# Split memory products in the convolution stage: one product between a tile's two pointwise units, two homes for the normed memory, other turns for the loads and taps

## The reference

```python
ff = silu(h2 @ w_ffn_gate) * (h2 @ w_ffn_up)            # 1024 -> 2816
x = x + ff @ w_ffn_down

def conformer_conv(h, ...):
    u = h @ w_pw1 + b_pw1                               # 1024 -> 2048
    a, gate = split(u, 2)
    u = a * sigmoid(gate)
    u = causal depthwise convolution of u, 31 taps, + b_dw
    u = silu(layernorm(u, ln_g, ln_b))
    return u @ w_pw2 + b_pw2

def memory_cross_attention(h, mem_n, ...):              # mem_n = rmsnorm(mem, norm_memsrc_g[layer])
    k = mem_n @ w_k                                     # 256 x 1024, for each of two layers
    v = mem_n @ w_v
    ...
```

## Time and profile before

| | us |
|---|---|
| median of 3 runs (lowest, highest) | 2284.11 (2280.6, 2284.97) |
| the profiled execution, its own time | 2286.37 |
| its span, first to last instruction | 2284.6 |
| PE busy | 2227.5 (98%) |
| DVE, ACT, POOL busy | 1341.9, 975.7, 403.4 |
| mean granted clock of PE | 0.991 |

### The profile page before, as it was taken

One profiled execution on the slowest core, in us unless ns is written; L12 is line 12 of the kernel. 1 busy time (PEld: TensorE's weight loads), 2 busy tenths in 40 slices (PEclk: granted clock), 3 DMA queues, 4 the chain that ended last, 5 costly groups with the idle time before them and its releaser, 6 DMA issues.

```text
span 2284.6 us, 31292 instructions
## 1 busy us (share of the span) xinstructions
PE 2227.5 (98%) x10692; PEld 1809.7 (79%) x10692; DVE 1341.9 (59%) x1900; ACT 975.7 (43%) x1490; POOL 403.4 (18%) x336
## 2 busy tenths in 40 slices
PE   8999999999999889889999999999999999999998
PEld 6787788888888677758888888887777888888887
DVE  5567757555545867865465445485555646454455
ACT  6775644433433556653342222245444333222222
POOL 2232102110010457624040000030000404000003
PEclk9999999999999999989999999999999999999999
DMA  4222223555666665532123333332221222333332
GB/s 147 65 65 63 76 83 93 161 188 184 198 191 216 192 197 184 169 127 66 57 81 101 93 101 93 92 93 79 59 63 56 84 65 83 101 92 95 99 95 89
DMA packets 413080, 253.36 MB, mean 111 GB/s; under 512 B 14832, under 2 KB 394224, under 8 KB 412976
## 3 DMA queue, kind: packets, MB, share of 16 engines
q1 hardware_dynamic: 412080, 249.68, 36.0%
q0 software_dynamic: 896, 2.33, 0.3%
HBM read 232.56 MB, written 18.87 MB: 110 GB/s over the span
## 4 chain that ended last, share of the span: by engine, by line
PE 85%; DVE 4%; POOLq 3%; issue 2%; ACT 2%; DMA 1%; DVEq 1%; SPq 0%; ACTq 0%; POOL 0%
PE bank L1944 24%; PE bank L1946 23%; PE bank L1945 23%; POOLq L674 3%; PE bank L1924 2%; DVE m_w_lo L1253 1%; PE bank L2415 1%; PE bank L2392 1%; PE bank L2097 1%; PE bank L2521 1%; PE bank L2488 1%; DVE bank L1649 1%; PE bank L2322 1%; PE bank L2235 1%; PE bank L2237 1%
## 5 line engine op out<-in xcount | busy, mean ns | idle before, releaser
L699 ACT ACTIVATE m_w_hi<-m_raw 128x1024 fp32r<-128x1024 f32 x332 | 351.3, 1058 | 817.4 <-PE bank L1946 802.1
L1944 PE MATMUL bank<-m_h_hi,m_w_hi 128*128 128x512 f32 x1504 | 607.0, 404 | 4.4 <-DVE m_w_lo L1253 2.3
L1946 PE MATMUL bank<-m_h_hi,m_w_lo 128*128 128x512 f32 x1504 | 587.0, 390 | 0.0
L1945 PE MATMUL bank<-m_h_lo,m_w_hi 128*128 128x512 f32 x1504 | 586.3, 390 | 0.0
L1253 DVE TENSOR_TENSOR m_w_lo<-m_raw,m_w_hi 128x1024 fp32r<-128x1024 f32 x332 | 449.0, 1352 | 125.9 <-ACT m_w_hi L699 121.8
L1944 PEld LDWEIGHTS bank<-m_h_hi,m_w_hi 128*128 128x128 f32 x1504 | 282.7, 188 | 76.0 <-issue 11.3
L1946 PEld LDWEIGHTS bank<-m_h_hi,m_w_lo 128*128 128x128 f32 x1504 | 282.3, 188 | 60.1
L1945 PEld LDWEIGHTS bank<-m_h_lo,m_w_hi 128*128 128x128 f32 x1504 | 282.9, 188 | 55.5 <-issue 2.4
L1944 PE MATMUL bank<-m_f_hi,m_w_hi 128*128 128x512 f32 x688 | 269.3, 391 | 3.2 <-DVE m_w_lo L1253 3.2
L1946 PE MATMUL bank<-m_f_hi,m_w_lo 128*128 128x512 f32 x688 | 267.9, 389 | 0.0
L1945 PE MATMUL bank<-m_f_lo,m_w_hi 128*128 128x512 f32 x688 | 267.8, 389 | 0.0
(11 more groups left out here) (399 smaller groups left out, 3256.5 us busy)
## 6 DMA issues: line engine op xcount, KB each, us to landing
m_raw<-in_ff_w SPq DMA_DIRECT2D x256, 256.0 KB, 3.0
mem_low<-m_mem_raw_lo SPq DMA_DIRECT2D x32, 512.0 KB, 3.9
m_mem_w_low<-mem_low SPq DMA_DIRECT2D x32, 512.0 KB, 5.2
m_raw<-in_conv_pw_w SPq DMA_DIRECT2D x48, 256.0 KB, 6.0
m_raw<-in_w_in SPq DMA_DIRECT2D x47, 256.0 KB, 3.3
m_raw<-in_w_ffn_gate SPq DMA_DIRECT2D x44, 256.0 KB, 3.2
m_raw<-in_w_ffn_up SPq DMA_DIRECT2D x44, 256.0 KB, 3.2
m_raw<-in_w_ffn_down SPq DMA_DIRECT2D x40, 256.0 KB, 3.1
```

The lines of the kernel that those rows point to most:

```text
L699: act.activation(WH[:, v % 2], RAW[:, v % 2], ACT.Copy).then_inc(s.w_hi, 1)
L1944: pe.matmul(o, high[:, r, k, :], hi, start=start, stop=False)
L1945: pe.matmul(o, high[:, r, k, :], lo, start=False, stop=False)
L1946: last = pe.matmul(o, low[:, r, k, :], hi, start=False, stop=stop)
```

## The change

On PE a tile's order becomes: unit A, its first memory unit, unit B, the other memory units, and the mean one place later. ACT, DVE and SP follow:

- ACT makes the high half of the first memory unit before unit A's step, those of the next two after it, and waits there for the first product to copy it out. The 8 high halves of layer 1's normed memory are made two in each of the tiles 1 to 4, behind the second half of the products. `m_mn_hi` has a buffer for each layer.
- DVE makes the low halves of layer 1 two in each of the tiles 1 to 4, between the step of A and the second run of taps; those of layer 0 all 8 after the last down pass. The taps run 9 and 9 instead of 8, 5 and 5, and `gated` stands before `tile_done`.
- The splits of the memory units end at unit 50 (`MEM_SPLIT_AT`): at units 4 to 14 by twos, 16 to 23 each, 24 to 38 by twos, 40 to 47 each, 48 and 50. SP stores a low half and loads the next raw block at one place.
- SP loads the first three memory units before the last down pass, has a ring of three slots and two more for units 30 and 31, and loads a tile's pointwise unit before the memory unit beside it.
- The last tile's taps: 18 on DVE, 10 on ACT and POOL, 3 on PE.

```diff
-SUM_TAPS_LAST = 8
+SUM_TAPS_LAST = 10
-MEM_SPLIT_FIRST = 4
+MEM_SPLIT_AT = (4, 6, 8, 10, 12, 14) + tuple(range(16, 24)) + tuple(range(24, 40, 2)) + tuple(range(40, 48)) + (48, 50)
-MEM_TURN = 5
-MEM_SLOT = [i % 4 for i in range(MEM_UNITS - 3)] + [2, 3, 4]
+MEM_SLOT = [i % 3 for i in range(MEM_UNITS - 2)] + [3, 4]
-PE_TAPS_LAST = 9
+PE_TAPS_LAST = 3
...
@@ sync: splits, loads
-            for i in range(MEM_UNITS):
-                split_at.setdefault(ffn + MEM_SPLIT_FIRST + 2 * i + 1, []).append(lambda i=i: split_in(i))
-                split_at.setdefault(ffn + MEM_SPLIT_FIRST + 2 * i + 6, []).append(lambda i=i: split_out(i))
+            for i, n in enumerate(MEM_SPLIT_AT):
+                split_at.setdefault(ffn + n + 5, []).append(lambda i=i: split_out(i))
+            for i, n in enumerate(MEM_SPLIT_AT):
+                split_at.setdefault(ffn + n + 3, []).append(lambda i=i: split_in(i))
...
+            def conv_loads(m, freed=()):
+                for half in range(2):
+                    if m < KD:
+                        unit(W["conv_pw1_w_2"][0], m * P + half * D)
+                    else:
+                        unit(W["conv_pw2_w_2"][0], half * P)
+                    for i in freed[:1] if half == 0 else freed[1:]:
+                        mem_load(i + 3)
...
-            for m in range(2, KD):
-                for i in range(*MEM_TILES[m - 2]):
-                    mem_load(i + 4)
-                conv_loads(m)
+            for m in range(2, KD + 1):
+                conv_loads(m, range(*MEM_TILES[m - 2]))
+            for i in (25, 26, 27, 30, 31, 28, 29):
+                if i == 30:
                     sp.wait_ge(s.unit_done, conv_done)
                 mem_load(i)
@@ scalar: conv_steps
                     products(m - 1, 0, SUM_TAPS // 2)
-                    mem_out(MEM_TILES[m - 1][1] - 1)
-                if m == MEM_TURN:
-                    act.wait_ge(s.mem_done, MEM_LAYER)
-                    for k in range(KD):
-                        memory_high(k, 1)
+                    mem_out(first - 1)
+                mem_high(first)
                 step(None)
-                for i in range(*MEM_TILES[m]):
+                for i in range(first + 1, min(last, first + 3)):
                     mem_high(i)
+                mem_out(first)
                 if m > 0:
                     products(m - 1, SUM_TAPS // 2, SUM_TAPS)
+                if 1 <= m <= 4:
+                    for k in range(2 * m - 2, 2 * m):
+                        memory_high(k, 1)
                 step(None)
@@ vector: conv_steps
-                cut = [0, 8, 13, DVE_TAPS]
+                cut = [0, 9, DVE_TAPS]
...
-                step(scaled(CA[:]), [chunk(0)] + ([memory_lows] if m == MEM_TURN else []))
+                step(scaled(CA[:]), [chunk(0)])
+                if 1 <= m <= 4:
+                    for k in range(2 * m - 2, 2 * m):
+                        memory_low(k, 1)
                 step(scaled(CG[:], None, s.cv_g), [chunk(1)])
-                chunk(2)()
+                gated()
                 if prev is not None:
                     tile_done(prev, DVE_TAPS)
-                gated()
@@ tensor: conv_units
+                first, last = MEM_TILES[m]
+                mem_product(first)
                 full(HH, HL)
-                for i in range(*MEM_TILES[m]):
+                for i in range(first + 1, last):
                     mem_product(i)
-                    if m >= 2 and i == MEM_TILES[m][0]:
+                    if m >= 2 and i == first + 1:
                         conv_mean(m - 2)
```

More of the change, by code:

```diff
@@ L516, in _ @@
                 if g0 == 16:
-                    for i in range(2):
+                    assert not split_at
+                    for i in range(3):
+                        sp.wait_ge(sw_io[i], 32 * ((MEM_UNITS - 1 - i) // 3 + 1))
+                    for i in range(3):
                         mem_load(i)
@@ L1059, in conv_steps @@
                     .then_inc(s.cv_sig, 1)
-                for i in range(MEM_TILES[m][0], MEM_TILES[m][1] - 1):
+                for i in range(first + 3, last):
+                    mem_high(i)
+                for i in range(first + 1, last - 1):
                     mem_out(i)
@@ L1072, in _ @@
                 conv_steps(m)
[L1073 to L1081 removed]
+            last = SUM_TAPS_LAST, PE_TAPS_LAST
+            products(KD - 1, 0, 4, *last)
+            mem_high(25)
+            mem_high(26)
+            mem_out(24)
+            products(KD - 1, 4, 7, *last)
+            mem_high(27)
+            products(KD - 1, 7, SUM_TAPS_LAST, *last)
+            mem_out(25)
+            mem_out(26)
+            mem_high(28)
+            mem_out(27)
+            mem_out(28)
+            for i in range(29, MEM_UNITS):
                 mem_high(i)
@@ L1096, in _ @@
                 act.activation(OH[:, k, :], (LY, CG)[k % 2][:], ACT.Copy).then_inc(s.ln_hi, 1)
-            for i in range(MEM_TAIL + 4, MEM_UNITS):
+            for i in range(29, MEM_UNITS):
                 mem_out(i)
@@ L1584, in split_low @@
             def split_low():
-                i, odd = divmod(U.n - 2 - ffn - MEM_SPLIT_FIRST, 2)
-                if odd or not 0 <= i < MEM_UNITS:
+                if U.n - 2 - ffn not in MEM_SPLIT_AT:
                     return
+                i = MEM_SPLIT_AT.index(U.n - 2 - ffn)
                 dve.wait_ge(s.sw_hi, i + 1)
@@ L2320, in mem_product @@
                     for k in range(KD):
-                        for a, b in ((high, MNH), (high, low_mn), (low, MNH)):
+                        for a, b in ((high, high_mn), (high, low_mn), (low, high_mn)):
                             last = pe.matmul(SBK[3][:, 0:MEM], a[:, k, :], b[:, k, :],
-                                             start=(k == 0 and a is high and b is MNH), stop=(k == KD - 1 and a is low))
+                                             start=(k == 0 and a is high and b is high_mn), stop=(k == KD - 1 and a is low))
                 else:
@@ L2330, in mem_product @@
                             c = slice(t * P, (t + 1) * P)
-                            for a, b in ((MNH, high), (MNH, low), (low_mn, high)):
+                            for a, b in ((high_mn, high), (high_mn, low), (low_mn, high)):
                                 last = pe.matmul(SBK[1 + t][:], a[:, k, c], b[:, j, :],
-                                                 start=(k == 0 and a is MNH and b is high),
+                                                 start=(k == 0 and a is high_mn and b is high),
                                                  stop=(k == KD - 1 and a is low_mn))
```

61 lines of the change are left out of this document (16 added, 45 removed).

## The result

The changed kernel takes 2303.07 us (2301.24 to 2306.29) against 2284.03 of the kernel before in the same measurement: a ratio of 1.0088 with a 95% interval of [1.007, 1.0105]. It is 19 us slower. The profiled execution has a span of 2302.0 us, 17.4 more than before.

The account below looks back on a forecast made before the run. The prediction took PE as the bound nearly everywhere; its terms, 4 − 4.6 − 1 + 8 − 11.4 − 1 = −6 us (tile 6: 0), off the median 2284.1 gave 2278, range 2264 to 2292.

Parts of the forecast that it names:

- Step 1: Feed-forward before its last down pass: store, raw load and up unit's load queued together cost +4 us (0 to +13).
- The rival of a slower feed-forward: The feed-forward's loads become its bound; with a landing of 7.5 us the time is 2294; chance 0.22.
- Step 2: Last down pass: low-half work leaves DVE, PE sets the pace at 32.6 us in place of 37.3; −4.6 us.
- Step 3: First tile: layer 0's low halves run at its start, PE waits 3.7 us for them; −1 us (−3 to +2).
- Step 4: Convolution tiles 1 to 5: DVE's taps wait behind the new halves, a loop turn takes 27.5 us; +8 (0 to +11).
- Step 5: Convolution tile 6: no wait before and no `m_mn_hi` behind its products now; 0 us.
- Step 6: Last tile: fewer PE taps and shorter waits, against a later high half for unit 25; −11 us (−16 to −5).
- The rival of no change: Tiles 1 to 5 loop at 28.5 us for late loads, last tile gives only 8 us; 2284 us, chance 0.27.

## Why the prediction was wrong

The forecast was 2278, within 2264 to 2292, faster at 0.45; the kernel took 2303. In the two steps that count the mechanism was the right one and the size was not: steps 1 and 4 were sized too small, and make up 20 of the 23 us between the sum as forecast (−6) and as measured (+17).

**Step 1, the feed-forward: +18.7 instead of +4.** This is the term that failed most. The chain was the right one; the overlap that the term took off it does not exist, and the landing is 0.5 us longer. SP's issues, then ACT, then DVE, over one cycle of the changed kernel (the start, the duration, what, and the idle time before with what ended it):

```profile
582.39 0.34 SPq L486 DMA_DIRECT2D mem_low<-m_mem_raw_lo  x1
582.77 0.43 SPq L477 DMA_DIRECT2D m_mem_raw<-in_mem_wk  x1
583.25 1.78 SPq L399 DMA_DIRECT2D m_raw<-in_w_ffn_up  x2
...
594.09 0.34 SPq L486 DMA_DIRECT2D mem_low<-m_mem_raw_lo  x1
```

```profile
589.48 1.06 ACT L692 ACTIVATE m_w_hi<-m_raw 128x1024 fp32r<-128x1024 f32 x1 [0.74 <-DMA m_raw<-in_w_ffn_up]
590.45 0.61 ACT L977 ACTIVATE m_f_hi<-m_f_full 128x512 fp32r<-128x512 f32 x1
```

```profile
591.10 0.69 DVE L1613 TENSOR_TENSOR m_f_lo<-m_f_full,m_f_hi 128x512 fp32r<-128x512 f32 x1 [2.57 <-ACT m_f_hi L977]
591.71 1.22 DVE L1255 TENSOR_TENSOR m_w_lo<-m_raw,m_w_hi 128x1024 fp32r<-128x1024 f32 x1
592.84 1.22 DVE L1591 TENSOR_TENSOR m_mem_raw_lo<-m_mem_raw,m_mem_raw_hi 128x1024 fp32r<-128x1024 f32 x1
```

From the store at 582.39 to the next at 594.09 are 11.7 us, where two units take PE 10.9. The load's `m_w_hi` starts at 589.48, 7.1 behind the store. Then everything stands in one line: `m_w_hi`, `m_f_hi`, `m_f_lo`, `m_w_lo`, `m_mem_raw_lo`, and 4.6 us later the next store. This is one of the shorter cycles. In the eleven with an up unit's load the 4.6 us never differ by more than 0.01, while `m_w_hi` starts 6.9 to 8.1 us behind the store, 7.5 on average, where the forecast had 7.0. A cycle is then 12.1. I had given both ends, 10.5 with the overlap and 11.8 without, and took a third of the way, reasoning that `m_f_hi` and `m_f_lo` are done while the load is on its way. They cannot be: `m_f_hi` stands behind `m_w_hi` in ACT's order, and `m_w_hi` waits for the load. The order could have settled it; averaging two ends did not. PE's turn is as long as the cycle: 12.0 us on average in the second pass (569.10 to 640.89 in six), and the six stores there are 12.0 apart too. That is 1.1 over PE's need, in 16 places and not 14, and makes nearly all of the 18.7. The 6.2 us in the busy column are inside these turns and no cost of their own.

The rival of a slower feed-forward was the one that came true, and it came near the point that its text names, a landing of 7.5 without overlap, which it prices at +20; but its reason was half wrong. The dense runs at 269 and 271 GB/s cost PE 1.1 us of idle time together in the changed kernel, and the sparse pairs, whose mean rate is far lower, cost the rest. The rule of the Trainium skill on "DMA: Bandwidth & Descriptors" (section "Anatomy of one DMA — SWDGE (gpsimd) path"), by which the three transfers would be in after an estimated 5.6 us, is for another path, and the trace does not agree with it on this one: 7.5 us on average.

**Step 2, the last down pass: −5.0 instead of −4.6,** right. The pass takes the 32.8 us that PE alone needs, and putting the low halves back costs 2.2 of the 5.0. DVE is left with 28.2 us of work and not 24, which is still less than PE's. That the splits make the rest was not tested by itself.

**Step 3, the first tile: +0.2 instead of −1.** The wait was 3.79, as sized (3.7), but at its end stood the high half behind the norm and not the low halves, as moving it showed. The eight low halves take 3.2 us there and not 5.3. That the number came out was luck.

**Step 4, tiles 1 to 5: +13.4 instead of +8,** the right mechanism with the first link of the loop too short. The chain in tile 2 of the changed kernel, from its first memory unit (PE) over ACT and DVE to that of tile 3:

```profile
852.50 0.80 PE L2332 MATMUL bank<-m_mem_w_high,m_mn_hi 128*128 128x512 f32 x1 [6.39 <-ACT m_mem_w_high L1007]
...
881.24 0.58 PE L2322 MATMUL bank<-m_mn_hi,m_mem_w_high 128*128 128x256 f32 x1 [5.65 <-ACT m_mem_w_high L1007]
```

```profile
854.96 1.06 ACT L1007 ACTIVATE m_mem_w_high<-m_mem_w 128x1024 fp32r<-128x1024 f32 x1 [1.56 <-DMA m_mem_w_low<-mem_low]
857.45 1.06 ACT L1007 ACTIVATE m_mem_w_high<-m_mem_w 128x1024 fp32r<-128x1024 f32 x1 [1.43 <-DMA m_mem_w_low<-mem_low]
...
865.03 0.89 ACT L965 ACTIVATE m_mn_hi<-m_mem_cols,m_vec 128x256 fp32r<-128x256 f32 x2
...
880.14 1.04 ACT L1007 ACTIVATE m_mem_w_high<-m_mem_w 128x1024 fp32r<-128x1024 f32 x1
```

```profile
865.56 1.98 DVE L1597 SCALAR_TENSOR_TENSOR m_mn_lo<-m_mem_cols,m_vec,m_mn_hi 128x256 fp32r<-128x256 f32 x2 [8.87 <-ACT m_mn_hi L965]
867.47 6.01 DVE L1649 SCALAR_TENSOR_TENSOR bank<-m_padded,m_vec,bank 128x512 f32<-128x512 f32 x9
...
875.34 0.75 DVE L1672 SCALAR_TENSOR_TENSOR m_padded<-m_conv_a,m_vec,m_conv_g 128x512 f32<-128x512 f32 x1
```

The working had, link by link: unit and copy 5.0, products 5.7 (from 859.36), high and low halves 1.7, taps 6.0, B to `m_padded` 2.8, six products 4.2, high half 1.4. The trace has 6.9, 5.7, 2.4, 5.9, 2.7, 4.0, 1.1, together 28.7. The first link is the one that grew, for two reasons. The working took the first memory unit for a key unit at half clock, 4.5. In the tiles 2 and 4 it is a value unit, and that takes 5.3. And the seven products stand behind the high halves of the next two units, which wait for their stored low halves to land: 1.56 and 1.43 us here, 2.65 and 1.65 in tile 3, where the unit is done 2.3 us before the second high half is. From the first memory unit to the products it is 6.9, 7.5 and 5.5 us in the tiles 2, 3 and 4, where I had 5.0 and up to 1.5. The low halves took 1.0 us each, while POOL was adding products, and not 0.66; in tile 0, with POOL idle, they took 0.40. With the turn at 28.9 on average, the term as I wrote it gives +12.4.

**Step 5, tile 6: +3.9 instead of 0.** The loop does not end with the last `m_mn_hi`: the first memory unit of tile 6 still waits 2.0 and runs at half clock, as tile 5 hands its lateness on. This is read from the trace and was not tested by itself.

**Step 6, the last tile: −13.4 instead of −11,** right in its size: the deal is worth 4.8 to 6.2 by the run that undid it, the wait for the squares 5.2 (8.2 to 3.0, as said), and the wait at unit 25 is 4.0 (said: 5). The 3 us that stay at the squares are not what the forecast took them for, POOL's two further additions: PE's last mean sets them, as said above. That number was luck.

The rival of no change put the loop at 28.5 for late loads. It was at 28.9, and late loads are a part of the reason. With the feed-forward cured the kernel came out at 2286, near the rival's 2284, but its other terms were not the rival's: it had +4 for the feed-forward and −8 for the last tile.

## What to carry to other kernels

- On an engine that works in order, an instruction that waits costs what stands behind it. Two low halves, 2 us in each of four tiles, cost some 26 us more ahead of nine taps than behind the tile's critical output. Ask of each new piece not how long it is but what is queued behind it, and what its own producer is queued behind.
- Where a chain's length lies between two ends and the bound in between, read from the order which operations can overlap, and do not average. The forecast had the right chain and then took two thirds of its cost off. A queue that releases load, store and load together turns separate latencies into one chain.
- Put a piece of background work where each schedule wants it: the store one place later cured the sparse schedule and hurt the dense one.

## What was unexpected in the hardware

- A wait of PE costs more than the idle time that the profile shows for it, at full clock too. With 16 waits the same 1354 to 1356 matmuls were busy for 310.8 us instead of 304.6 at a granted clock of 1.00. Of the 0.39 us a wait, 0.16 is how the profile books the row in front of it, and 0.10 is the slower second matmul behind it. Curing some 10 us of such waits gave 14.4 us of time, and curing 12.3 gave 17.
- The mean data rate said little of the waits: 269 GB/s over 45 us with 1.0 us of idle PE, but 175 GB/s over 84 us with 5.0, in the changed kernel:

```profile
524.00:569.00 45.00, 44.03 (x192) 35.45 (x190) 25.16 (x27) 16.96 (x17) 1.54 (x2) 1.00 0.87 269
569.00:653.00 84.00, 79.05 (x338) 62.83 (x338) 43.10 (x50) 32.04 (x37) 0.00 (x0) 1.00 0.64 175
```
